# First two tiles of each down stage computed chunk by chunk together, in the first and last feed-forward too

## The reference, cut to what matters

```python
def half_ffn(h, g, shift, scale, gate, w_gu, w_down):
    return h + 0.5 * gate * swiglu(norm_mod(h, g, shift, scale), w_gu, w_down)
def swiglu(x, w_gu, w_down):          # D_FF = 2816
    gt, up = jnp.split(x @ w_gu, 2, axis=-1)
    return (jax.nn.silu(gt) * up) @ w_down
```

## Time and profile before

| what | value |
|---|---|
| median of three runs | 3440.08 us (3439.55 to 3441.85) |
| the profiled execution's own time | 3442.58 us |
| its span | 3440.8 us |
| TensorE matmuls (PE) busy | 3312.9 us, 96% |
| weight loads (PEld) busy | 3059.2 us, 89% |
| VectorE (DVE) busy | 2310.1 us, 67% |
| ScalarE (ACT) busy | 1220.8 us, 35% |
| GpSimd (POOL) busy | 70.3 us, 2% |
| DMA | 308.86 MB, mean 90 GB/s |
| mean granted TensorE clock | 0.989 |

### The profile page before, as it was taken

How to read it: one execution, slowest core, us unless ns; L and a number is a source line. 1 busy time by engine, 2 the same in 40 slices (tenths; PEclk the granted TensorE clock), 3 DMA queues, 4 the chain that set the end, 5 groups by cost and what they waited for, 6 DMA issues and landing times.

```text
span 3440.8 us, 46472 instructions
## 1 busy us (share of the span) xinstructions
PE 3312.9 (96%) x18292; PEld 3059.2 (89%) x18292; DVE 2310.1 (67%) x3854; ACT 1220.8 (35%) x2057; POOL 70.3 (2%) x178
## 2 busy tenths in 40 slices
PE   8999999999999999989999989989999999999989
PEld 6999999988989999989999989978888888877777
DVE  5979895567687777787777766654334766455654
ACT  4111113255543343453433333452222332334332
POOL 0000000000000000000000000000000000000000
PEclk9999999999999999999999999999999999999999
DMA  5545553110122222212222221113332310222232
GB/s 206 184 176 178 180 183 103 66 31 19 38 68 68 92 86 87 85 40 75 82 75 98 92 87 54 48 50 98 98 96 94 120 47 19 73 70 67 61 96 95
DMA packets 93545, 308.86 MB, mean 90 GB/s; under 512 B 11232, under 2 KB 15520, under 8 KB 91792
## 3 DMA queue, kind: packets, MB, share of 16 engines
q1 hardware_dynamic: 88128, 290.04, 25.2%
q0 software_dynamic: 5200, 15.83, 1.4%
HBM read 300.06 MB, written 4.19 MB: 88 GB/s over the span
## 4 chain that ended last, share of the span: by engine, by line
PE 47%; DVE 6%; ACT 2%; issue 1%; DMA 0%; POOL 0%; DVEq 0%; ACTq 0%
PE psum L666 30%; PE psum L1083 9%; PE psum L2743 1%; PE psum L3093 1%; PE psum L2722 1%; DVE h L749 1%; PE psum L1811 1%; DVE rawl L646 1%; PE psum L3102 1%; PE psum L1828 0%; PE psum L3106 0%; ACT wh L636 0%; PE psum L1709 0%; DVE sw_s L1860 0%; PE psum L2731 0%
## 5 line engine op out<-in xcount | busy, mean ns | idle before, releaser
L666 PE MATMUL psum<-zh,wh 128*128 128x384 f32 (+2 forms) x2384 | 780.8, 373 | 43.2 <-DVE sx L3593 17.6
L666 PE MATMUL psum<-zh,rawl 128*128 128x384 f32 (+2 forms) x2384 | 753.2, 361 | 0.0
L666 PE MATMUL psum<-zl,wh 128*128 128x384 f32 (+2 forms) x2384 | 753.1, 361 | 0.0
L636 ACT ACTIVATE wh<-raw 128x512 fp32r<-128x512 f32 (+3 forms) x551 | 447.3, 817 | 841.7 <-PE psum L666 443.9
L646 DVE TENSOR_TENSOR rawl<-raw,wh 128x512 fp32r<-128x512 f32 (+3 forms) x551 | 502.7, 927 | 292.4 <-ACT wh L636 291.4
L666 PEld LDWEIGHTS psum<-zh,wh 128*128 128x128 f32 x2384 | 441.2, 191 | 102.2 <-issue 40.4
L1083 PE MATMUL psum<-formq,wh 128*128 128x386 f32 x1848 | 480.3, 341 | 17.4 <-DVE rawl L646 10.7
L666 PEld LDWEIGHTS psum<-zh,rawl 128*128 128x128 f32 x2384 | 442.5, 191 | 43.3
L666 PEld LDWEIGHTS psum<-zl,wh 128*128 128x128 f32 x2384 | 443.2, 191 | 41.3 <-issue 2.9
L1083 PEld LDWEIGHTS psum<-formq,wh 128*128 128x128 f32 x1848 | 337.7, 190 | 23.2 <-DVE rawl L646 13.6
L749 DVE SCALAR_TENSOR_TENSOR h<-psum,mod,h 128x512 f32<-128x512 f32 (+1 forms) x288 | 170.0, 628 | 185.9 <-PE psum L666 185.8
(11 more groups left out here) (485 smaller groups left out, 4758.1 us busy)
## 6 DMA issues: line engine op xcount, KB each, us to landing
raw<-in_wup SPq DMA_DIRECT2D x176, 512.0 KB, 3.9
modw<-in_mod_w SPq DMA_DIRECT2D x128, 512.0 KB, 3.7
raw<-in_w_sw SPq DMA_DIRECT2D x36, 512.0 KB, 3.5
raw<-in_wdn SPq DMA_DIRECT2D x64, 256.0 KB, 3.9
raw<-in_wdn SPq DMA_DIRECT2D x32, 448.0 KB, 3.2
adaw<-in_ada_w SPq DMA_DIRECT2D x8, 1024.0 KB, 15.1
raw<-in_wdn SPq DMA_DIRECT2D x16, 512.0 KB, 4.0
raw<-in_od_in SPq DMA_DIRECT2D x16, 512.0 KB, 3.7
```

The costliest lines, as they stand in the source:

```text
L636: nc.scalar.activation(hi_of(n, i), x, ACT.Copy).then_inc(w_hi, 1)
L666: last = nc.tensor.matmul(psum[:, at + to:at + to + e - s], w[:, q * P:(q + 1) * P], x[:, q, s:e], start=(q == 0 and j == 0), stop=(q == s ...
```

## The change

One keyword of one call in ffn_pe. The down stages of ffn0 and ffn3 are called with ready in place of own_ready; six stages, three in each.

```diff
@@ -1060,7 +1060,7 @@
                     products(pe, up, zh, zl, **beside_first(pe, k))
                 else:
                     products(pe, up, zh, zl, ready=lambda q: pe.wait_ge(n_z, OPERAND_SPLITS[k] + q + 1))
-                products(pe, down, hidh, hidl, own_ready=lambda q: pe.wait_ge(hid_done, pairs + q + 1))
+                products(pe, down, hidh, hidl, ready=lambda q: pe.wait_ge(hid_done, pairs + q + 1))
```

## The result

| | before | changed |
|---|---|---|
| median | 3438.62 us | 3445.41 us |
| lowest to highest | 3434.55 to 3443.86 | 3439.97 to 3449.04 |
| executions | 17 | 17 |
| mean | 3438.94 us | 3444.68 us |

The ratio is 1.0016 (95% interval 1.0010 to 1.0023): the changed kernel is slower, by 5.75 ± 1.75 us in the means and 6.8 us in the medians. 8.9 us more and a time of 3449.0 had been forecast, with 3446.5 as the low end. The direction is right, the time is 3.6 us too high and outside the range. Of these, 1.5 us are the starting point: the median of 3440.08, to which the sum was added, came from three executions, and 17 give 3438.62. The other 2.1 us (3.2 by the means) are missing from the sum, and most of this document is about where they went.

A forecast was written before the change was run, and what follows sets the result against it. TensorE, busy 96% of the span, was taken to lose time only where it stands still. Waits of 5.8 and 3.1 us, with later work costed at nothing, gave 8.9 us on the 3440.08 median: 3449.0 us, range 3446.5 to 3451.5.

The forecast's parts named there:

- (a): Six down stages: tile 1 waits for its PSUM half after one chunk; 1.50 us each in ffn0, 0.44 in ffn3, 5.8 us.
- (b): Pair's end in six down stages: third tile waits for tile 0's residual; 0.52 us each in ffn0, 0.50 in ffn3, 3.1 us.
- (c): After tile 0 in the down stages: first residual about 7 us late on VectorE, costed at nothing because later work has cover.
- The thinnest cover: ffn3's last down stage: second residual releases 0.9 us before the fourth tile is wanted, so no stall.
- The absorbed case: Even mixer behind ffn0: a self-timed wait, GpSimd's 2.3 us, swallows delay; 6.6 us more, 3446.7 us; chance 0.08.
- The clock rival: New waits in ffn0 lower TensorE's granted clock; 5.1 us on top if all three do, 3454.1 us; chance 0.05.

The follow-up runs named there:

- e9: Changed kernel, but in the six down stages tile 0, then tile 1, runs three chunks alone before alternating; 1.32 ± 1.84 us against the kernel before.
- e1: Kernel before with the pairing in ffn0's three down stages alone; median 3446.12 against 3440.11 us, ratio 1.0020.
- e10: Changed kernel with three leading chunks for each tile and tile 0's last two chunks ahead of tile 1's; 0.87 ± 2.10 us against the kernel before.
- e3: Kernel before, old order, with repeated matmuls adding 2.09 us of work in each of ffn0's three down stages; 5.42 ± 1.43 us, ratio 1.0017.
- e2: Kernel before with the pairing in ffn3's three down stages alone; median 3439.54 us, ratio 1.0000.
- e5: Second measurement of the kernel before with the pairing in ffn3's three down stages alone; ratio 1.0002.
- e6: Kernel before, old order, with 13 repeated matmuls (2.95 us) in ffn3's last down stage; 1.52 ± 1.47 us, ratio 1.0005.
- e13: Kernel before, old order, with 13 repeated matmuls (2.95 us) in gates_swa, behind the windowed attention; 1.50 ± 2.02 us, ratio 1.0003.
- e12: Kernel before, tile 0's last two chunks together in eight ffn1/ffn2 down stages, two leading chunks in ev_qkv and dn_in; median 3434.17 against 3440.12 us, ratio 0.9984.

## Why the prediction was right and wrong

**What bounds the kernel** was read rightly for the six stages: the order of the matmuls decided which wait was last. For the program it was read too narrowly. "So time is lost only where TensorE stands still" leaves out the time at the lower clock, though the mean granted clock of 0.989 over 3440.8 us is 0.011 x 3440.8 = 38 us of clock. The sum below inherits this.

**(a) Tile 1's wait for its PSUM half, 5.8 us: right.** The three waits of 1.26 us and three of 0.2 are there, and e9 removes them and with them all but (b). The size hangs on when VectorE reaches the freeing operation: in e1's trace the first of them is 1.56. The point that made this exact was to take release, latency and the slower first matmuls as three terms, each from a row of another place in the same kernel.

**(b) The end of the pair, 3.1 us: right.** Six more waits for L749 of 0.28 (5.2 us in all, 5.4 had been said), 0.50 to 0.56 us for each stage in e9, none in e10.

**(c) Whoever follows tile 0, nothing: right.** The thinnest cover was ffn3's last down stage; its fourth tile's split starts 2656.70 - 2653.80 = 2.90 us after the residual (2.91 in the earlier trace rows), and the stage lost 0.99 us like the other two. In ffn0 VectorE stood for 7.46 us (about 7 had been said) and had caught up by its fourth residual.

**The sum carried to the end: wrong.** "Sum: 5.8 + 3.1 = 8.9 us more" is right for the six stages (9.06) and wrong as a step to the program's time. It took for granted that each microsecond lost in a stage arrives at the end, unless a wait that runs by its own time absorbs it. ffn0's 6.1 us do arrive, to within the intervals (e1, e3). ffn3's 2.95 don't (e2, e5: -0.22 ± 1.20), though no wait absorbs them: in the trace the lag is 7.2 us from dn_in to 2940, and falls only where the granted clock differs. The term that was put at nothing is the time at the lower clock behind the edit, which differs between the kernels and between executions of one kernel by several parts of about 1.7 us. Of the 3.6 us by which the forecast time was too high, 2.1 are this and 1.5 the starting point.

**The rivals.** The absorbed case named a place, the even mixer, and GpSimd's wait. That wait is 2.4 us in the new trace (2.3), so nothing went into it. That its time, 3446.7, came nearer to the measured one than the forecast is luck. The clock rival asked the wrong question. It looked at the new waits and found rightly that they lower nothing: 1.00 throughout ffn0, and a busy delay costs the same as a standing one to within 2.1 us. The Trainium skill (TensorE: Matmul & The Clock Gate, "A second HAM failure mode: psum-queue depth-cycling") tells of a kernel that changes PSUM banks in each iteration and whose clock swings because TensorE idles briefly and often between groups. The trace shows no such swing behind the new waits of 1.26 and 0.28 us, but six of them in 610 us are few, so it doesn't test the case in which they come often. What should have been asked is how much the stretches of lower clock that the kernel already has elsewhere differ from kernel to kernel and from run to run. The earlier trace rows showed one of them, worth 1.7 us; two more or fewer are over a third of the forecast.

**The size of the anchor.** The median of three executions lay 1.5 us above that of 17, while single executions of one kernel spread over 9 us (3434.55 to 3443.86). A range of 2.5 us to each side held this, or the missing 2 us, but not both.

**What stays open.** Why the stretches of lower clock fall as they do, and whether the delay moves them. In the means a delay of 1.4 us in front of the second block comes with a program some 2 us faster and 3.4 with one as much slower as the delay is long; between them, at 2.95, e6 and the pair e2 and e5 differ by 1.7 us (1.52 ± 1.47 against -0.22 ± 1.20), not surely. The runs show that the missing time goes with the clock, but neither by which rule nor that lateness is the cause. Whether a delay behind the windowed attention arrives in full is open too (e13).

## What to carry to other kernels

Computing two tiles chunk by chunk together makes them want their buffers at once and hand them back at once; give the first tile two or three chunks of its own at the start and two at the end, and the waits for the buffers go away, provided that the engine which frees them is idle by then (all of them in e10's six stages, 6 of 13 in e12). Price a local stall from exact neighbours in the trace, but give the program's time as that price plus or minus a few of the stretches of lower clock which the kernel already has; here two of them, 3.4 us, would have covered the miss. Where a few microseconds in thousands are at stake, measure a plain delay of the same size at the same place before believing that an edit there gained or lost anything.

## What the runs showed of the hardware

- Added work needn't make a program slower: 1.36 us of repeated matmuls ahead of the second block gave -2.11 ± 1.23 us (two runs of 11; ratios 0.9995 and 0.9992, with 1 inside either interval), at a granted clock higher by 0.8 to 1.3 thousandths.
- One part at 1.2 GHz costs about 1.7 us here, and 0.9 in one place where TensorE waits in it (3140 to 3155). Executions of the identical program differ in it: the same matmul of ffn1 came 4.38 and 8.02 us later than in the trace of before, with the same losses in the edited stages ahead of it, and ffn3 started from 4.85 us earlier to 2.34 us later in eight traces that have the same program up to there.
- TensorE standing (e1: 6.4 us in three waits of 1.26 to 1.56 and three of 0.28) and TensorE working (e3: 3 x 2.09 us of repeated matmuls) cost the same to within the intervals, 6.36 ± 1.77 and 5.42 ± 1.43 us, and the granted clock stays at 1.00 around such waits.
